# One-core transformer block: inputs loaded first, an eviction moved up, and rotary encoding done on the projection's chunks

## The reference

```
mod = silu(c) @ w_ada + b_ada                 # 6 parts of 2048: sh1, s1, g1, sh2, s2, g2; once for x, once for the context
h  = rmsnorm(x)   * norm1_w * (1 + s1)  + sh1
hc = rmsnorm(ctx) * norm1_w * (1 + s1c) + sh1c       # 256 context tokens, same weights
p  = h @ w_in          # -> q_da, k_da, v_da (1024 each), c_q (384), c_kv (256), k_rope (64); the same for hc
q_mla = rmsnorm(c_q) @ w_uq ;  kv = rmsnorm(c_kv) @ w_ukv
q_da, k_da, q_rope, k_rope of x are rotated (axial rotary, groups of 64 columns); those of the context are not
o  = attention of 8 "da" heads (two softmaxes, subtracted) and 8 "mla" heads over 512 keys (context, then x)
x  = x + g1 * (merge(o) @ w_o)
x  = x + g2 * conv_ffn(modulate(rmsnorm(x)))
```

## Time and profile before

| | |
|---|---|
| median of 3 runs | 2899.01 us (2896.28 to 2901.13) |
| the profiled execution | 2893.64 us, of which its span 2892.0 us |
| PE busy | 2795.1 us, 97% of the span |
| DVE, ACT, POOL busy | 60%, 43%, 6% |
| first projection and start | 0 to 427 us |
| attention of the first block | 427 to about 550 us |

### The profile page before, as it was taken

The page is one execution under the profiler, slowest core; times in us unless marked ns, Lnnn a source line. Parts: engine busy times, 40 slices in busy tenths (PEclk is TensorE's granted clock), DMA queues, the critical chain, the costliest instruction groups (busy, mean ns, idle before and its releaser), DMA issues.

```text
span 2892.0 us, 34207 instructions
## 1 busy us (share of the span) xinstructions
PE 2795.1 (97%) x13474; PEld 2288.1 (79%) x13474; DVE 1737.4 (60%) x1857; ACT 1232.5 (43%) x1345; POOL 172.6 (6%) x340
## 2 busy tenths in 40 slices
...
GB/s 379 322 344 253 344 264 178 275 269 154 210 174 156 216 224 183 180 158 206 209 226 240 240 241 211 216 189 205 93 193 214 189 189 189 185 177 204 169 173 152
DMA packets 348573, 621.43 MB, mean 215 GB/s; under 512 B 49792, under 2 KB 102672, under 8 KB 340896
## 3 DMA queue, kind: packets, MB, share of 16 engines
...
## 4 chain that ended last, share of the span: by engine, by line
PE 90%; DVE 4%; DMA 3%; ACT 2%; issue 1%; SPq 0%; POOL 0%; DVEq 0%; ACTq 0%; POOLq 0%
PE ps L309 23%; PE ps L311 23%; PE ps L310 23%; PE ps L1202 3%; PE ps L1204 3%; PE ps L1203 3%; PE ps L426 1%; DVE w_lo L271 1%; PE ps L1879 1%; PE ps L1488 1%; DMA k_in<-proj 1%; PE ps L326 0%; PE ps L325 0%; PE ps L324 0%; DMA raw<-in_w_ada 0%
## 5 line engine op out<-in xcount | busy, mean ns | idle before, releaser
L271 DVE TENSOR_TENSOR w_lo<-raw,w_hi 128x2048 fp32r<-128x2048 f32 (+3 forms) x428 | 896.7, 2103 | 671.0 <-ACT w_hi L264 669.9
L264 ACT ACTIVATE w_hi<-raw 128x2048 fp32r<-128x2048 f32 (+3 forms) x428 | 747.2, 1757 | 733.9 <-PE ps L311 684.2
L309 PE MATMUL ps<-w_hi,a_hi 128*128 128x512 f32 x2240 | 876.9, 391 | 3.4 <-DVE a_lo L806 2.7
L311 PE MATMUL ps<-w_hi,a_lo 128*128 128x512 f32 x2240 | 872.2, 389 | 0.0
L310 PE MATMUL ps<-w_lo,a_hi 128*128 128x512 f32 x2240 | 871.6, 389 | 0.0
L309 PEld LDWEIGHTS ps<-w_hi,a_hi 128*128 128x128 f32 x2240 | 420.6, 188 | 90.3 <-DVE a_lo L806 3.3
L311 PEld LDWEIGHTS ps<-w_hi,a_lo 128*128 128x128 f32 x2240 | 420.5, 188 | 87.7
L310 PEld LDWEIGHTS ps<-w_lo,a_hi 128*128 128x128 f32 x2240 | 420.8, 188 | 85.5
L309 PE MATMUL ps<-w_hi,b_hi 128*128 128x512 f32 x796 | 312.2, 392 | 3.8 <-DVE b_lo L845 3.8
L311 PE MATMUL ps<-w_hi,b_lo 128*128 128x512 f32 x796 | 310.5, 390 | 0.0
L310 PE MATMUL ps<-w_lo,b_hi 128*128 128x512 f32 x796 | 310.4, 390 | 0.0
...
## 6 DMA issues: line engine op xcount, KB each, us to landing
...
```

Source lines behind the costliest of these rows:

```text
L264: nc.scalar.activation(w_hi[s][:, 0:n_k, 0:ncols], raw[s][:, 0:n_k, 0:ncols], ACT.Copy).then_inc(sem("hi_done"), 1)
L271: nc.vector.tensor_tensor(w_lo[s][:, 0:n_k, 0:ncols], raw[s][:, 0:n_k, 0:ncols], w_hi[s][:, 0:n_k, 0:ncols].bitcast(F32), ALU.subtract).th ...
L309: nc.tensor.matmul(o, h, w_hi[s][:, k, 0:ncols], start=kt == 0, stop=False)
L311: last = nc.tensor.matmul(o, l, w_hi[s][:, k, 0:ncols], start=False, stop=kt == L.groups[-1][0] + L.groups[-1][1] - 1)
```

## The change

1. The DMA queue loads x, the identity and the context ahead of the first modulation weight. The transposes of x follow the first `ada_first`, those of the context the second. The context's scaling moves from ACT to DVE, and the first quarter of piece 0 is multiplied after ada 9 instead of 10.
2. K0 is evicted at position 9 instead of 10, with fewer late units ahead of it; `LATE_AFTER` is dealt out anew, and Q0 goes ahead of V0.
3. q and k are rotated once by POOL as whole chunks in `stg[0]` (7 instructions a chunk, over 128x512 for each of two token tiles), and ACT stores the rotated rows. In the attention the da heads are no longer rotated, only q of the mla heads.
4. x's second load and the loads of the g2 weights move from the attention's start to heads 4 to 7.

```diff
-        LATE_AFTER = [0] * 7 + [7, 3, 3, 3, 3, 3, 3, 4, 3, 2, 2, 2, 3, 2, 1, 3, 2, 0, 2, 0, 0, 2, 3, 3, 3, 3, 2,
-                                3, 5, 5, 5, 5, 6]
+        LATE_AFTER = [0] * 7 + [3, 0, 3, 3, 3, 5, 5, 5, 5, 1, 2, 1, 2, 2, 2, 2, 2, 0, 1, 0, 1, 6, 6, 6, 6, 1, 1, 1, 2, 5, 5, 5, 4]
...
         def ada_sp(sp):
             sp.dma_start(condr[:], A["pack_cond"]).then_inc(sem("cond_in"), 16)
+            for t in range(TILES):
+                sp.dma_start(X[:, t, :], A["x"][0, t * P:(t + 1) * P, :]).then_inc(sem("x_in"), 16)
+            sp.dma_start(ident[:], A["const_ident"]).then_inc(sem("cols_in"), 16)
+            for t in range(TILES):
+                sp.dma_start(ctx_in[t][:], A["ctx"][0, t * P:(t + 1) * P, :]).then_inc(sem("ctx_in"), 16)
             ada_load(sp, 0)
...
             for n in range(8):
                 ada_first(pe, n)
-                if n == 2:
-                    for f in range(KT // 2):
+                if n < 2:
+                    for f in range(n * KT // 2, (n + 1) * KT // 2):
                         z_flip(pe, f)
...
-            steps = {n: (q, n - first) for q, first in enumerate((10, 19, 27)) for n in range(first, first + 8)}
+            steps = {n: (q, n - first) for q, first in enumerate((9, 18, 26)) for n in range(first, first + 8)}
...
-            ("lat_kv", W_IN, OFF_CKV, KV_RANK + ROPE, True, PROJ), ("in", W_IN, OFF_V, CHUNK, True, PROJ),
-            ("in", W_IN, 0, CHUNK, False, PROJ_X), *[("uk", W_UKV, n * CHUNK, CHUNK, True, PKV) for n in range(4)],
+            ("lat_kv", W_IN, OFF_CKV, KV_RANK + ROPE, True, PROJ), ("in", W_IN, 0, CHUNK, False, PROJ_X),
+            ("in", W_IN, OFF_V, CHUNK, True, PROJ), *[("uk", W_UKV, n * CHUNK, CHUNK, True, PKV) for n in range(4)],
...
+        ROTATED = (K0, KL, Q0, len(CHUNKS) - 3, len(CHUNKS) - 2)
...
-            return ENDS[j] + (2 if CHUNKS[j][0] in SHORT else 3)
+            return ENDS[j] + (2 if j == K0 or CHUNKS[j][0] in SHORT else 3)
...
-            if X_STORED[j]:
+            if j - 1 in ROTATED and j - 1 != KL:
+                act.wait_ge(sem("rotated"), ROTATED.index(j - 1) + 1)
+            elif X_STORED[j]:
                 act.wait_ge(sem("stored_x"), 16 * X_STORED[j])
...
+        def rotate_chunk(pool, chain, j):
...
+            for t in range(TILES):
+                def halves(v, h):
+                    return v.rearrange("p (g b h f) -> p g b h f", b=2, h=2, f=16)[:, :, :, h, :]
+                for h in range(2):
+                    s_h = rope_s[:, t, :].rearrange("p (b h f) -> p b h f", h=2, f=16)[:, :, h, :]
+                    last = nc.gpsimd.tensor_tensor(halves(swapped[:, t, :], h), halves(x[:, t, :], 1 - h),
+                                                   s_h.unsqueeze(1).to_broadcast([P, n_g, 2, 16]), ALU.mult)
+            chain.done(last)
+            for t in range(TILES):
+                v = x[:, t, :].rearrange("p (g n) -> p g n", n=ROPE)
+                last = nc.gpsimd.tensor_tensor(v, v, rope_c[:, t, :].unsqueeze(1).to_broadcast([P, n_g, ROPE]), ALU.mult)
+            chain.done(last)
+            out = x if j == KL else swapped
+            nc.gpsimd.tensor_tensor(out, x, swapped, ALU.add).then_inc(sem("rotated"), 1)
...
             for h in range(2):
                 att_load_v(sp, h)
-            for kt in range(4):
-                g2_load(sp, kt)
-            gate_bias_load(sp, 1)
-            x_again(sp)
...
                 att_load_v(sp, h)
-                while loaded < G2_ATT and loaded < g2_rows(2 * h - 2) + RING:
+                if h in (4, 5):
+                    x_again(sp, h - 4)
+                if h in (6, 7):
+                    for kt in range(2):
+                        g2_load(sp, 2 * (h - 6) + kt)
...
+        def att_flip(pe, h, i=None):
+
+            par = h % 2
             if h < HEADS:
+                pe.wait_ge(sem(f"at_qk_in{par}"), 32 * (h // 2 + 1))
```

More of the change, by code:

```diff
@@ L478, in z_flip @@
                 pe.wait_ge(sem("norm_diag"), 1)
+                pe.wait_ge(sem("cols_in"), 16 * 6)
             if f == KT // 2:
[L480 removed]
+                pe.wait_ge(sem("norm_diag"), 2)
             if f >= Z_BANKS:
@@ L530, in ada_pe @@
                     ada_total(pe, 0)
-                if n == 5:
-                    for f in range(KT // 2, KT):
-                        z_flip(pe, f)
             ada_total(pe, 1)
-            steps = {n: (q, n - first) for q, first in enumerate((10, 19, 27)) for n in range(first, first + 8)}
+            steps = {n: (q, n - first) for q, first in enumerate((9, 18, 26)) for n in range(first, first + 8)}
             for n in range(8, N_FIRST):
                 ada_first(pe, n)
+                if n % RING == 0 and n > 8:
+                    ada_total(pe, n // RING - 1)
                 if n in steps:
                     dense(*steps[n])
-                if n % RING == 0 and n > 8:
-                    ada_total(pe, n // RING - 1)
-            dense(2, 5)
             ada_total(pe, N_ADA - 1)
@@ L554, in ada_act @@
             norm_stats_act(act, "n1", [X[:, t, :] for t in range(TILES)], D, 0)
-            for f in range(KT // 2):
-                z_copy(act, f)
             act.wait_ge(sem("ctx_in"), 32)
             norm_stats_act(act, "n1c", [ctx_in[t][:] for t in range(TILES)], D, 2)
-            act.wait_ge(sem("norm_diag"), 2)
-            for t in range(TILES):
-                nc.scalar.activation(ctx_in[t][:], ctx_in[t][:], ACT.Copy, scale=stat[:, 2 + t:3 + t]).then_inc(sem("ctx_in"), 1)
-            for f in range(KT // 2, KT):
+            for f in range(KT):
                 z_copy(act, f)
@@ L576, in x_scale, with x_again @@
             last.then_inc(sem("norm_diag"), 1)
-        def x_again(sp):
-            sp.wait_ge(sem("flip_t"), KT)
-            for t in range(TILES):
-                sp.dma_start(X[:, t, :], A["x"][0, t * P:(t + 1) * P, :]).then_inc(sem("x_in"), 16)
+        def x_again(sp, t):
+            if t == 0:
+                sp.wait_ge(sem("flip_t"), KT)
+                sp.wait_ge(sem("mod_stored"), 16)
+            sp.dma_start(X[:, t, :], A["x"][0, t * P:(t + 1) * P, :]).then_inc(sem("x_in"), 16)
         def ada_dve(dve, chain):
@@ L1002, in store_act @@
             first = KV_RANK if kind == "lat_kv" else 0
-            x_rows = dst[SEQ:2 * SEQ] if both else dst
-            act.dma_start(tok(x_rows[:, c0 + first:c0 + w]), stg[0][:, :, first:w]).then_inc(sem("stored_x"), 16)
+            if j not in ROTATED:
+                x_rows = dst[SEQ:2 * SEQ] if both else dst
+                act.dma_start(tok(x_rows[:, c0 + first:c0 + w]), stg[0][:, :, first:w]).then_inc(sem("stored_x"), 16)
             if both:
```

91 lines of the change are left out of this document (53 added, 38 removed).

## The result

The changed kernel takes 2911.23 us (median of 6 runs, 2908.11 to 2916.43), the kernel before beside it 2897.78: a ratio of 1.0050 (95% interval 1.0039 to 1.0061), 13.5 us **slower**. The forecast was 9 us faster, with a range that ended at 2900. The profiled execution took 2909.04 us (span 2907.3).

The account below looks back on a forecast made before the run. PE was taken as the bound, busy for 2795.1 of 2892.0 us, so only its waits could shrink. The terms +0.8 - 0.5 + 3 - 12.4 gave -9.1 us, 2890 on the median, with a range of 2878 to 2900.

Parts of the forecast that it names:

- Step 1: At the start, up to the first dense matmul: it comes at about 46.5 for 55.82, -9.2 us (-6 to -10).
- Step 2: At piece 8: PE's 12.0 us wait for K0's eviction goes, and the piece starts at 138.2 instead of 159.34.
- Step 3: DVE's stretch to c_kv's scaling takes 66.5 us; PE waits 15.5 and about 6 at pieces 14, 15; piece 20 +0.8.
- Step 4: Pieces 20 to 39: +2.5 us, from -0.5 at evictions and stores and +3 in K1.
- The term for K1: From K1 to Q1, 16.5 million bytes must come in 45 us; PE waits 0 to 6 us, taken as +3.
- Step 5: In the attention: moved loads and POOL out of the path give -12.4 us (range -10 to -12.4).
- DMA paces the late units, and it is slower: Rival for the late-unit stretches: below some 325 GB/s loads hold DVE up, +7 us, 2906; chance 12%.

Follow-up runs that it names:

- experiment 11: The changed kernel with the same 27 late units ahead of c_kv's scaling, but never more than four behind a piece: 1.0031 of the kernel before.
- experiment 12: The changed kernel with the same 29 units behind pieces 28 to 35, but 4, 4, 4, 4, 4, 3, 3, 3 behind them: 1.0011 of the kernel before.
- experiment 7: The kernel before with only x's second load and the g2 weights moved to heads 4 to 7, POOL still rotating each head: 0.9956, 2887.3 us.
- experiment 5: The kernel before with the new start alone (inputs first, context scaled by DVE, first quarter of piece 0 after ada 9): 0.9982.
- experiment 6: The kernel before with K0 evicted at position 9, the new LATE_AFTER and Q0 ahead of V0, no rotation in the projection: 1.0078.

## Why the prediction was wrong

**Step 1, -9.2: mis-sized, -4.4.** The first dense matmul came at 47.9 (46.5 forecast). "From there the same 91.6 us of work follow" failed: it was 95.1, since with the first quarter of piece 0 after ada 9 one group more of modulation lies behind it, PE's clock was at 0.63 from 47.8 to 52 us, and one more wait of 0.9 us for DVE came. Piece 7's subtraction, on which step 3 counts, ended at 133.6 (127.4 forecast), only 3.1 us earlier than before: DVE's work ahead of it came 4.2 us earlier, and 1.2 were lost to piece 7's weights, for which ACT and then DVE waited. Alone the start was worth 5 us.

**Step 2, K0's wait: right.** No wait at piece 8; it came at 143.0 for 138.2, by what step 1 lacked.

**Step 3, the mechanism right, one term wrong.** The waits moved to pieces 14 and 15 as written (20.3 and 6.1 for 15.5 and 6), and from the scaling to piece 20 it was 69.4 us for 69. The rotation cost 4.1 to 4.8 for 4. What failed is "Before, DVE waited 6.6 us for units in this stretch; I take half of it now, -3". It waited 9.2, so the stretch was 71.5, just beyond its bound, and not 66.5. The reason, from experiment 11: I had reckoned bytes against GB/s, while the wait comes from the count behind a piece, for at most four units behind each took it from 9.2 to 1.9. With 6.2 us from step 1 and 5.0 here the scaling was 11.2 late, and piece 20 at 274.5 for 262.9.

**Step 4, +2.5: the largest miss, +12.4.** From piece 20 to 28 it was -4.5 (-0.5 forecast). Of these, 2.1 are the second w_ukv piece's wait, 3.3 us before and 1.2 now: its accumulator had stood behind the store of Q0. Another 1.8 are PE's own work there, 37.1 us at a granted clock of 0.96 before and 35.4 at 1.00 now. Pieces 28 to 39 took 131.2 us for 114.2: +17 for +3. The term for K1 failed: the step asked only whether 16.5 million bytes come in 45 us, and not when the fifth load of a piece is issued. Both windows, of before and of after:

```profile
309.30:423.50 114.20, 114.20 (x513) 94.69 (x514) 84.41 (x64) 24.30 (x15) 29.52 (x36) 0.99 0.87 313
```

```profile
317.12:448.30 131.18, 121.14 (x513) 98.13 (x514) 93.30 (x67) 24.10 (x15) 28.05 (x14) 0.93 0.82 285
```

Of the 17 us 10 are waits for subtractions, the longest 5.65, and 7 are the same 513 matmuls at a lower granted clock. In the second profile of the changed kernel they are 13.8 and 5.4. Dealing out the same 29 units with four at most behind a piece (experiment 12) took the stretch to 118.8 us.

**Step 5, -12.4: right, -11.** Step u = 5 to 6 fell by 10.2 (10.3 forecast), u = 6 to 15 by 1.0 (1.7), u = 0 to 5 by 1.1, and behind u = 15 1.2 came back. Its cause was named rightly, the loads, and experiment 7 shows that the rotation was hardly needed for it.

The sum: 12.4 to piece 20, 12.4 to the end of the projection and -11 in the attention are 13.8; at the first matmul of w_o it is 13.4, and the span is 15.3 longer. The other 2 us, behind the attention, stay open. Nor do the parts add up alone: experiments 5, 6 and 7 give -5, +23 and -13 us, +5 in all, where the changed kernel lost 13.5. The rotation and a start whose gain ends in c_kv's wait are in the difference; how much each has was not taken apart. The rival "DMA paces the late units, and it is slower" had the sign and half of the size (+7), but not the cause: it turned "below some 325 GB/s". The rate did lie below that (285 over pieces 28 to 39), but because the loads were issued late: with four at most behind a piece, 362 were to be had.
